# A transformer pair in split fp32r: moving the start addresses of the turned activations and of the fp32r tensors

## The chip, the cores and the metric

The kernel runs on one core of one Trainium2 chip. The metric is the time of one execution on the device in microseconds, as the median of several executions. Distances between addresses are given in bytes within a partition of SBUF.

## The reference

Two transformer layers on 256 tokens of width 1024, all in fp32. Cut to what matters here:

```python
def first_block(x, ...):                      # layer 1
    h = x
    h = h + 0.5 * swiglu(rms_norm(h, ffn1_norm), ffn1_w_gu, ffn1_w_down)      # ffn_a
    h = h + hybrid_mixer(rms_norm(h, mix_norm), w_in, ..., w_out)             # NSA and HGRN2
    h = h + 0.5 * swiglu(rms_norm(h, ffn2_norm), ffn2_w_gu, ffn2_w_down)      # ffn_b
    return rms_norm(h, final_norm)
def swiglu(x, w_gu, w_down):
    gate, up = jnp.split(x @ w_gu, 2, axis=-1)                                # width 2752
    return (jax.nn.silu(gate) * up) @ w_down
# second_block: two layers of FFN, attention (first FoX, then MLA), FFN (ffn_c to ffn_f),
# each followed by a layer norm, and a gated per-layer embedding behind each layer
```

## The kernel before

**Numbers.** Each matmul in fp32 is made of three in fp32r: an operand is split in a high part (a rounded copy) and a low part (the rest), and hi·hi, hi·lo and lo·hi are summed in PSUM. Weights come by DMA in chunks of 128 x 3072 floats into four buffers `w_raw`; ScalarE writes the high part into one of two buffers `w_hi` (line 407), VectorE the low part into one of two `w_lo` (line 414).

**Turned activations.** There are norm stages n = 0 to 11. After each but the last, TensorE turns the 256 x 1024 activations (line 492), ScalarE writes the high parts (line 736) and VectorE the low parts (line 849). Stages 0 to 7, 9 and 10 all write the same tensor `xT`, of 8 k-tiles x (high, low) x 256 tokens, so a k-tile's high and low part stand side by side (2,048 bytes); stage 8 writes `o2_hi`, `o2_lo` (`mla_oT`). An FFN f = a to f reads the stage n = 0, 2, 3, 5, 7, 9; the mixer's projections read n = 1, FoX n = 4, the gates of the embeddings n = 6 and 10, MLA's shared keys n = 7; MLA keeps the outputs of heads 0 to 7 in `xT`.

**What TensorE does with it.** The stationary operand is loaded by an instruction of its own ahead of its matmul; the other operand moves.

- FFN, tiles 1 to 20 of 22 (and tile 0 for c, d, e): `feature_major_twice`, once for gate and once for up. Weights are stationary, `xT` moves. Per k: `lo` weights against the high part (256 columns, line 451, or 454 for k = 0), and `hi` weights against high and low together (512 columns, line 452). So one tile is 16 matmuls of 512 columns and 16 of 256, which alternate. Then come the 12 matmuls of 512 columns of the tile before it that multiply by w_down (`token_major`, line 462): `hT_hi` or `hT_lo` is stationary, weights move. Late tiles of b to f put off half of this and use copies, `held_w_*` and `held_hT_*`.
- `feature_major` (line 441): weights stationary, 256 columns of `xT`, or of `mla_cqT`/`mla_ckvT`, move. It serves the projections of the mixer, FoX and MLA and the last tile of each FFN.
- `token_major` (line 462) with `xT`, `mix_oT`, `fox_oT`, `mla_oT` stationary, weights moving: output projections, gates, values.
- `block_tokens`, `pe_first` and `first_tile` (lines 506 to 513, 564 to 568, 588 to 591): the first products behind a norm.

**Order.** Each engine runs its own list, written out by hand (`pe_program` and the like), with semaphores between them.

**Where tensors lie.** They are placed one behind another in the order of declaration, each padded to 32 bytes: 4 `w_raw`, 2 `w_hi`, 2 `w_lo` (12,288 bytes each), `x`, `xn` (8,192 each), `xT` (16,384), `gains` (8,192), `const` (11,008), three of 1,024, then `hT_hi0`, `hT_hi1`, `hT_lo0`, `hT_lo1` (1,024 each), five small ones (160 bytes with their padding), `small` (256), and behind that what each stage brings of its own: `mix_oT_*` or `fox_oT_*` first; in MLA `ckvT_hi`, `ckvT_lo` (2,048 each), `k_rope` (1,024), the gains (2,560), `stat` (32), `oT_hi`, `oT_lo` (8,192 each), `cqT_hi`, `cqT_lo` (3,072 each). The held copies begin 29,824 bytes behind `hT_lo1`: `held_w_hi`, `held_w_lo` (8,192 each), `held_between` (776 floats), four `held_hT_*`.

Of the kernel before, what the change touches and what calls it, by code (L numbers as in the profile page):

```python
# [246 lines left out]


def build(nc, t, out):
    with ExitStack() as ctx:  # L250
# [40 lines left out]
        xT = sb("xT", [P, KD, 2, SEQ], F32R)  # L291
        xT_hi, xT_lo = xT[:, :, 0, :], xT[:, :, 1, :]
# [21 lines left out]
        small = sb("small", [P, 64])  # L314
# [130 lines left out]
        def feature_major_twice(o, hi, lo, col):  # L445
# [49 lines left out]
        def pe_first(n, src, i, tiles):  # L495
# [3 lines left out]
            front, back = range(KD // 2), range(KD // 2, KD)  # L499

# [70 lines left out]
        def pe_ffn(f, n, src):  # L571

            at = first[FFN[f]]

# [19 lines left out]
            def gate_up(i):  # L594
# [91 lines left out]
        def pe_features(i, tiles, signal, a_hi=None, a_lo=None, k_tiles=KD, n=None, col=None):  # L686

            hi, lo = w_hi[chunks[i].pair], w_lo[chunks[i].pair]
            wait_split(pe, i)
            for j, (o, free) in enumerate(tiles):  # L690
                pe.wait_ge(*free)
                feature_major(o, hi, lo, col or (lambda k: (len(tiles) * k + j) * P), k_tiles, a_hi or xT_hi, a_lo or xT_lo,
                              range(k_tiles)).then_inc(signal, 1)

        def pe_tokens(i, width, tiles, signal):

            wait_split(pe, i)
# [6 lines left out]
        def act_squares(n, src, mean, blocks=range(TB)):  # L704

            for b in blocks:
                for half in range(2):
# [9 lines left out]
                    elif n in PLE_NORM:  # L717
                        aside = xT_hi[:, 4 * half:4 * half + 4, tok_of(b)]
# [7 lines left out]
        def turned_views(n, p):  # L726
# [3 lines left out]
            return [z[:, k0:k0 + 4, tok_of(b)] for z in ((o2_hi, o2_lo) if n == 8 else (xT_hi, xT_lo))] + [bank[:, :].rearrange("p (k t) -> p k t", t=P)]  # L730
# [318 lines left out]
        def pe_mixer():  # L1049
# [3 lines left out]
            pe_tokens(first["nsa_v"], VSW, [(bank(3, VSW), none), (bank(4, VSW), none)], mix_tile)  # L1053
            pe_tokens(first["hg_g"], SEQ, [(bank(5), none), (bank(6), none)], mix_tile)
            pe_tokens(first["hg_g"] + 1, SEQ, [(bank(7), none), (bank(0), (nsa_copied, 1))], mix_tile)
# [16 lines left out]
            pe_features(place["hg_fq", 0], [(bank(2), (nsa_copied, 3)), (bank(3), (nsa_copied, 4))], mix_tile)  # L1072
            pe_features(place["hg_fq", 1], [(bank(4), (nsa_copied, 5)), (bank(5), (gate_made_hg, 1))], mix_tile)
            compressed(0)
            pe_features(place["hg_fq", 2], [(bank(6), (gate_made_hg, 2)), (bank(7), (gate_made_hg, 3))], mix_tile)
            compressed(1)
            pe_features(place["hg_fq", 3], [(bank(0), (gate_made_hg, 4)), (bank(2), (fk_sig_made, 1))], mix_tile)
            compressed(2)
            pe_tokens(place["hg_v", 0], SEQ, [(bank(3), (q_made, 1)), (bank(4), (fk_sig_made, 2))], mix_tile)
            compressed(3)  # L1080
            pe_tokens(place["hg_v", 1], SEQ, [(bank(5), (q_made, 2)), (bank(6), (fk_sig_made, 3))], mix_tile)
            pe_features(first["nsa_b"], [(bank(7), (q_made, 3)), (bank(0), (fk_sig_made, 4)), (bank(2), (q_made, 4))], mix_tile)
# [7 lines left out]
            pe_features(first["nsa_c"], [(bank(4), (hv_copied, 2)), (bank(5), (hv_copied, 3))], mix_tile)  # L1090
# [585 lines left out]
        def pe_fox():  # L1676
            none = (fox_tile, 0)

            f, v = first["fox_f"], first["fox_v"]
            pe_turn(4, x, (0, 1))  # L1680
# [4 lines left out]
            pe_features(f, [(psum[4][:, 0:SEQ], none)], fox_tile)  # L1685
            block_tokens(4, v + 1, SEQ, psum[3][:, 0:SEQ], 1, xT_hi, xT_lo).then_inc(fox_tile, 1)
            tiles = lambda f0, f1: [(psum[7][:, 0:SEQ], f0), (psum[6][:, 0:SEQ], f1)]
            pe_tokens(v + 2, SEQ, tiles(none, none), fox_tile)
# [4 lines left out]
            pe_tokens(first["fox_v"] + 3, SEQ, tiles((fox_v_made, 5), (fox_v_made, 6)), fox_tile)  # L1693
# [185 lines left out]
        with ExitStack() as scope:  # L1879
# [6 lines left out]
            lat_stat = lt("stat", [P, 2 * TB, 2])  # L1886
# [24 lines left out]
        def mla_out(h):  # L1911
            hi, lo = (xT_hi, xT_lo) if h < KD else (o2_hi, o2_lo)
            return hi[:, h % KD, :], lo[:, h % KD, :]

        def pe_shared_kv():

            pe_tokens(first["kv_down1"], KL, [(psum[b][:, 0:KL], (added, 4 * 7 + 2)) for b in range(TB)], mla_tile)
            pe_turn(8, x, (0, 1))
            pe_features(first["kv_down2"], [(psum[2 + j][:, 0:SEQ], (added, 4 * 7 + 4)) for j in range(2)], mla_tile)
            pe_turn(8, x, (2, 3))  # L1920

        def pe_mla():
# [88 lines left out]
            def rest(c, b, half):  # L2011
# [9 lines left out]
                if b == 0:  # L2021
                    pe.wait_ge(att_lo, A0 + min(3 * c + 3, MLA_H))

            pe_out(("mla_o1", "mla_o2"), lambda h: (xT_hi if h < KD else o2_hi)[:, h % KD, :],
                   lambda h: (xT_lo if h < KD else o2_lo)[:, h % KD, :], MLA_H, 3, ahead=rest)
# [644 lines left out]
```

## Time and profile before

| | |
|---|---|
| time, median of 3 executions | 1739.42 us (1739.07 to 1739.47) |
| profiled execution, first to last instruction (its span) | 1736.7 us |
| PE busy | 1674.9 us (96% of the span) |
| DVE busy | 1185.4 us (68%) |
| ACT busy | 873.0 us (50%) |
| HBM read and written | 173 GB/s over the span |

The profile is of one execution; of its own time only the span is given, and what lies before the first and behind the last instruction is not in it. PE is TensorE's matmuls, PEld its weight loads, DVE VectorE, ACT ScalarE, POOL GpSimd. The end of a matmul is modelled, so that a matmul's duration reaches over the start of the next. What a matmul costs in a stream is therefore the distance from its start to the start of the next one; in the chain of waits, which gives to each instruction only its part of the path, a row "x12" with 2.72 us says just that of twelve.

### The profile page before, as it was taken

Reading aid. Unit: us, or ns where it says so; the run is one execution under the profiler, and the core shown is the slowest. Engines: PE = TensorE matmul, PEld = TensorE weight load, DVE = VectorE, ACT = ScalarE, POOL = GpSimd, SP = SyncE. Lnnn points to the kernel's source line nnn. Section 1 sums busy time; section 2 is a strip of 40 time slices with the busy share of each in tenths; the row PEclk is TensorE's granted clock in tenths of the full one; section 3 lists DMA queues with packets and bytes.
Section 4 is the critical chain, followed back from the end, with each engine's and each line's share of the span. In section 5 each row is a group of like instructions: output and inputs, shape, how many; then the busy total and the mean of one; then the engine's idle time right before and its main releaser. Section 6 shows DMA issues by size and latency. Waiting matters only on the chain.

```text
span 1736.7 us, 24477 instructions
## 1 busy us (share of the span) xinstructions
PE 1674.9 (96%) x9836; PEld 1450.7 (84%) x9836; DVE 1185.4 (68%) x1949; ACT 873.0 (50%) x1497; POOL 76.0 (4%) x115
## 2 busy tenths in 40 slices
PE   7999999999999999999999999989999999999997
PEld 6888798888888888888878888778889887888885
DVE  5666646966666776675877667766667675576676
ACT  4544455655444544445655444544445565454444
POOL 0000002201000000001200000000000000100000
PEclk9999999899999999999999999999999999999999
DMA  8545255024555455445436554545445333455541
GB/s 347 190 182 186 107 201 237 1 97 170 185 194 199 174 208 192 182 146 219 146 146 229 198 196 171 193 174 185 182 176 203 117 113 119 162 222 200 189 158 49
DMA packets 32113, 301.57 MB, mean 174 GB/s; under 512 B 3824, under 2 KB 4352, under 8 KB 6016
## 3 DMA queue, kind: packets, MB, share of 16 engines
q1 hardware_dynamic: 32000, 300.01, 46.6%
q8 instruction: 78, 1.28, 0.3%
q14 instruction: 35, 0.29, 0.1%
HBM read 298.93 MB, written 1.06 MB: 173 GB/s over the span
## 4 chain that ended last, share of the span: by engine, by line
PE 86%; DVE 7%; ACT 5%; issue 1%; POOL 0%; DMA 0%; SPq 0%; DVEq 0%; ACTq 0%
PE bank L462 29%; PE bank L452 26%; PE bank L451 11%; PE bank L441 8%; DVE w_lo L414 3%; PE bank L454 2%; ACT w_hi L407 1%; PE bank L589 1%; PE bank L492 1%; PE bank L1155 1%; PE bank L1106 1%; DVE xT L849 1%; PE bank L1123 0%; DVE x L819 0%; ACT bank L721 0%
## 5 line engine op out<-in xcount | busy, mean ns | idle before, releaser
L414 DVE TENSOR_TENSOR w_lo<-w_raw,w_hi 128x1024 fp32r<-128x1024 f32 (+5 forms) x535 | 593.9, 1159 | 215.0 <-ACT w_hi L407 214.3
L452 PE MATMUL bank<-xT,w_hi 128*128 128x512 f32 x1920 | 674.2, 396 | 0.6 <-DVE w_lo L414 0.6
L407 ACT ACTIVATE w_hi<-w_raw 128x1024 fp32r<-128x1024 f32 (+5 forms) x543 | 507.9, 995 | 115.6 <-PE bank L462 93.5
L451 PE MATMUL bank<-xT,w_lo 128*128 128x256 f32 x1680 | 468.5, 279 | 0.0
L452 PEld LDWEIGHTS bank<-xT,w_hi 128*128 128x128 f32 x1920 | 351.8, 188 | 70.4 <-DVE w_lo L414 1.0
L451 PEld LDWEIGHTS bank<-xT,w_lo 128*128 128x128 f32 x1680 | 316.9, 189 | 10.5
L767 ACT ACTIVATE ff_silu<-ff_silu 128x256 f32<-128x256 f32 x123 | 51.5, 419 | 390.6 <-DVE ff_silu L917 390.6
L462 PE MATMUL bank<-w_hi,hT_hi 128*128 128x512 f32 x488 | 190.6, 391 | 0.5 <-DVE hT_lo L926 0.5
L462 PE MATMUL bank<-w_hi,hT_lo 128*128 128x512 f32 x488 | 189.9, 389 | 0.0
L462 PE MATMUL bank<-w_lo,hT_hi 128*128 128x512 f32 x488 | 189.9, 389 | 0.0
L917 DVE TENSOR_REDUCE ff_silu<-bank 128x256 f32<-128x512 f32 x123 | 84.9, 690 | 106.5 <-PE bank L452 105.1
L441 PE MATMUL bank<-xT,w_hi 128*128 128x256 f32 x672 | 123.6, 285 | 1.0 <-DVE w_lo L414 1.0
L462 PE MATMUL bank<-w_hi,xT 128*128 128x256 f32 (+2 forms) x448 | 107.9, 334 | 6.7 <-ACT mla_v L2053 2.6
L441 PEld LDWEIGHTS bank<-xT,w_hi 128*128 128x128 f32 x672 | 104.8, 191 | 5.7 <-issue 4.2
L462 PEld LDWEIGHTS bank<-w_hi,hT_lo 128*128 128x128 f32 x488 | 91.6, 188 | 19.7
L462 PEld LDWEIGHTS bank<-w_lo,hT_hi 128*128 128x128 f32 x488 | 91.6, 188 | 19.7
L462 PEld LDWEIGHTS bank<-w_hi,hT_hi 128*128 128x128 f32 x488 | 91.6, 188 | 15.6 <-issue 1.3
L441 PE MATMUL bank<-xT,w_lo 128*128 128x256 f32 x336 | 95.0, 283 | 0.0
L926 DVE TENSOR_TENSOR hT_lo<-ff_silu,hT_hi 128x256 fp32r<-128x256 f32 x122 | 51.9, 425 | 59.0 <-ACT hT_hi L773 59.0
L773 ACT ACTIVATE hT_hi<-ff_silu 128x256 fp32r<-128x256 f32 x122 | 50.9, 417 | 78.9 <-DVE ff_silu L924 78.9
L462 PEld LDWEIGHTS bank<-w_hi,xT 128*128 128x128 f32 x448 | 75.4, 190 | 16.3 <-issue 4.6
L918 DVE TENSOR_REDUCE ff_up<-bank 128x256 f32<-128x512 f32 x123 | 83.7, 680 | 0.0
(388 smaller groups left out, 2221.3 us busy)
## 6 DMA issues: line engine op xcount, KB each, us to landing
w_raw<-in_ffn_a SPq DMA_DIRECT2D x22, 1536.0 KB, 6.7
w_raw<-in_ffn_b SPq DMA_DIRECT2D x22, 1536.0 KB, 6.5
w_raw<-in_ffn_c SPq DMA_DIRECT2D x22, 1536.0 KB, 6.5
w_raw<-in_ffn_d SPq DMA_DIRECT2D x22, 1536.0 KB, 6.5
w_raw<-in_ffn_e SPq DMA_DIRECT2D x22, 1536.0 KB, 6.4
w_raw<-in_ffn_f SPq DMA_DIRECT2D x22, 1536.0 KB, 6.3
gains<-in_gains SPq DMA_DIRECT2D x11, 1024.0 KB, 4.8
w_raw<-in_mla_up SPq DMA_DIRECT2D x8, 1280.0 KB, 5.7
```

Source lines behind the costliest of these rows:

```text
L407: nc.scalar.activation(hi, src, ACTF.Copy).then_inc(w_hi_made, 1)
L414: nc.vector.tensor_tensor(lo, src, hi.bitcast(F32), ALU.subtract).then_inc(w_lo_made, 1)
L441: ins = nc.tensor.matmul(o, w[:, c], a[:, k, :], start=(n == 0), stop=(n == last))
L451: nc.tensor.matmul(o[:, 0:SEQ], lo[:, c], xT[:, k, 0, :], start=False, stop=False)
L452: ins = nc.tensor.matmul(o, hi[:, c], xT[:, k, :, :], start=(k == 0), stop=(k == KD - 1))
L454: nc.tensor.matmul(o[:, 0:SEQ], lo[:, c], xT[:, k, 0, :], start=False, stop=False)
L462: ins = nc.tensor.matmul(o, a(k)[:, tok_of(b)], w[:, c], start=(first_k and n == 0), stop=(last_k and n == 3 * len(ks) - 1))
L767: nc.scalar.activation(sig[s][r, :], gate[r, :], ACTF.Silu).then_inc(silu_made, 1)
L773: nc.scalar.activation(hT_hi[z][r, :], sig[s][r, :], ACTF.Copy).then_inc(h_hi_made, 1)
L917: nc.vector.tensor_reduce(sig[s][:, :], gate.rearrange("p (two s) -> p s two", two=2), AX_X, ALU.add).then_inc(gate_summed, 1)
L918: m = dve_own.step(nc.vector.tensor_reduce(up_sum[:, :], up.rearrange("p (two s) -> p s two", two=2), AX_X, ALU.add))
L926: nc.vector.tensor_tensor(hT_lo[z][r, :], sig[s][r, :], hT_hi[z][r, :].bitcast(F32), ALU.subtract).then_inc(h_lo_made, 1)
```

## The change

`xT` becomes a room of 128 floats more, and each stage n takes its own view of the room, `TURNED_AT[n]` floats behind the room's start: 64 bytes for n = 0, 128 for n = 2, 192 for n = 1, 3, 4, 6 and 10, 256 for n = 5, 320 for n = 7, 384 for n = 9. All that reads or writes `xT` takes the view of its stage; MLA's heads 0 to 7 take that of n = 9. The tensors behind the room move by 512 bytes. `small` grows by 32 bytes, `held_between` by 32, `lat_stat` by 32, so that `mix_oT`, `fox_oT`, `ckvT`, `held_hT`, the embeddings' `pT` copies, `mla_oT` and `cqT` begin at multiples of 64 bytes. No instruction is added, removed, resized or put at another place, and no wait changes.

```diff
+TURNED_AT = {0: 16, 1: 48, 2: 32, 3: 48, 4: 48, 5: 64, 6: 48, 7: 80, 9: 96, 10: 48}
+TURNED_ROOM = 128
...
-        xT = sb("xT", [P, KD, 2, SEQ], F32R)
-        xT_hi, xT_lo = xT[:, :, 0, :], xT[:, :, 1, :]
+        xT_room = sb("xT", [P, 2 * KD * SEQ + TURNED_ROOM], F32R)
+        def turned_x(n):
+            a = TURNED_AT[n]
+            return xT_room[:, a:a + 2 * KD * SEQ].rearrange("p (k two s) -> p k two s", k=KD, two=2)
+        def turned_hi_lo(n):
+            return turned_x(n)[:, :, 0, :], turned_x(n)[:, :, 1, :]
...
-            sb("held_between", [P, 776], on=held)
+            sb("held_between", [P, 784], on=held)
...
-        small = sb("small", [P, 64])
+        small = sb("small", [P, 72])
...
-                    feature_major_twice(gate, hi, lo, lambda k: 2 * P * k)
-                    feature_major_twice(up, hi, lo, lambda k: 2 * P * k + P).then_inc(gate_up_made, 1)
+                    feature_major_twice(gate, hi, lo, lambda k: 2 * P * k, turned_x(n))
+                    feature_major_twice(up, hi, lo, lambda k: 2 * P * k + P, turned_x(n)).then_inc(gate_up_made, 1)
...
-            lat_stat = lt("stat", [P, 2 * TB, 2])
+            lat_stat = lt("stat", [P, 2 * TB, 4])
...
-            hi, lo = (xT_hi, xT_lo) if h < KD else (o2_hi, o2_lo)
+            hi, lo = turned_hi_lo(9) if h < KD else (o2_hi, o2_lo)
```

## Rows read from the trace of the kernel before

**Rows 1.** The page: busy time of the engines, and PE's largest matmul groups.

```profile
PE 1674.9 (96%) x9836; PEld 1450.7 (84%) x9836; DVE 1185.4 (68%) x1949; ACT 873.0 (50%) x1497; POOL 76.0 (4%) x115
...
L452 PE MATMUL bank<-xT,w_hi 128*128 128x512 f32 x1920 | 674.2, 396 | 0.6 <-DVE w_lo L414 0.6
L451 PE MATMUL bank<-xT,w_lo 128*128 128x256 f32 x1680 | 468.5, 279 | 0.0
```

**Rows 2.** The chain that ended last, whole span, by line.

```profile
by line: PE bank L462 28.8%; PE bank L452 25.8%; PE bank L451 11.3%; PE bank L441 8.1%; DVE w_lo L414 2.8%; PE bank L454 1.6%; ACT w_hi L407 1.3%; PE bank L589 1.1%; PE bank L492 0.8%; issue 0.8%; PE bank L1155 0.6%; PE bank L1106 0.5%; DVE
```

**Rows 3.** Windows of ffn_b, ffn_c and FoX: stretch, its length, each engine's busy time.

```profile
core 0: us, PE busy (x) PEld busy (x) DVE busy (x) ACT busy (x) POOL busy (x), PEclk, DMA share, GB/s
410.00:584.00 174.00, 173.70 (x946) 149.81 (x944) 119.09 (x150) 82.49 (x111) 0.00 (x0) 1.00 0.53 197
606.00:765.00 159.00, 159.00 (x846) 136.40 (x845) 110.46 (x136) 75.74 (x99) 0.00 (x0) 1.00 0.51 184
828.00:865.00 37.00, 37.00 (x308) 32.93 (x304) 30.25 (x86) 25.69 (x76) 11.14 (x20) 1.00 0.48 171
```

**Rows 4.** The chain in order of time, an FFN tile's down part, twice: start, us, what.

```profile
438.04 2.72 PE bank L462 x12
446.35 2.72 PE bank L462 x12
```

**Rows 5.** Timeline of PE, gate (from 440.60) and up (from 443.41) of one tile.

```profile
440.60 0.39 PE L452 MATMUL bank<-xT,w_hi 128*128 128x512 f32 x1
440.82 0.28 PE L454 MATMUL bank<-xT,w_lo 128*128 128x256 f32 x1
...
443.18 0.63 PE L452 MATMUL bank<-xT,w_hi 128*128 128x512 f32 x2
443.65 0.28 PE L454 MATMUL bank<-xT,w_lo 128*128 128x256 f32 x1
...
446.19 0.39 PE L462 MATMUL bank<-w_hi,hT_hi 128*128 128x512 f32 x1
```

**Rows 6.** The chain: streams of 256 columns with `xT` moving (mixer, FoX, ffn_d's last tile).

```profile
238.82 11.52 PE bank L441 x96
828.33 3.07 PE bank L441 x24
1081.28 5.75 PE bank L441 x48
```

**Rows 7.** Timeline of PE: a stream of 256 columns with `mla_cqT` moving, first and tenth.

```profile
1401.08 0.28 PE L441 MATMUL bank<-mla_cqT_hi,w_lo 128*128 128x256 f32 x1
...
1402.10 0.28 PE L441 MATMUL bank<-mla_cqT_hi,w_lo 128*128 128x256 f32 x1
```

**Rows 8.** The chain: 512 columns, stationary `mix_oT`, `fox_oT`, `held_hT` mostly, `xT` with `mla_oT`.

```profile
386.86 16.11 PE bank L462 x69
891.84 14.26 PE bank L462 x60
1087.03 11.25 PE bank L462 x48
1471.94 25.42 PE bank L462 x111
```

**Rows 9.** The waits of PE: line waited for, us in total, times, longest.

```profile
PE bank L589 <- DVE xT L849: 10.1, 6, 5.2
PE bank L482 <- DMA const<-in_const: 8.5, 1, 8.5
PE bank L506 <- DVE w_lo L414: 4.8, 3, 1.8
```

More of the change, by code:

```diff
@@ L443, in feature_major, with feature_major_twice @@
             return ins
-        def feature_major_twice(o, hi, lo, col):
+        def feature_major_twice(o, hi, lo, col, xT):
             for k in range(KD):
@@ L691, in pe_features, with pe_tokens @@
                 pe.wait_ge(*free)
-                feature_major(o, hi, lo, col or (lambda k: (len(tiles) * k + j) * P), k_tiles, a_hi or xT_hi, a_lo or xT_lo,
-                              range(k_tiles)).then_inc(signal, 1)
-        def pe_tokens(i, width, tiles, signal):
+                feature_major(o, hi, lo, lambda k: (len(tiles) * k + j) * P, KD, xT_hi, xT_lo, range(KD)).then_inc(signal, 1)
+        def pe_tokens(n, i, width, tiles, signal):
+            xT_hi, xT_lo = turned_hi_lo(n)
             wait_split(pe, i)
@@ L728, in turned_views @@
             k0, bank = 4 * half, psum[4 + 2 * b + half]
-            return [z[:, k0:k0 + 4, tok_of(b)] for z in ((o2_hi, o2_lo) if n == 8 else (xT_hi, xT_lo))] + [bank[:, :].rearrange("p (k t) -> p k t", t=P)]
+            return [z[:, k0:k0 + 4, tok_of(b)] for z in ((o2_hi, o2_lo) if n == 8 else turned_hi_lo(n))] + [bank[:, :].rearrange("p (k t) -> p k t", t=P)]
         def act_turn(n, pieces=range(4)):
@@ L1679, in pe_fox @@
             f, v = first["fox_f"], first["fox_v"]
+            xT_hi, xT_lo = turned_hi_lo(4)
             pe_turn(4, x, (0, 1))
@@ L1692, in pe_fox @@
             ins.then_inc(cum_turned, 1)
-            pe_tokens(first["fox_v"] + 3, SEQ, tiles((fox_v_made, 5), (fox_v_made, 6)), fox_tile)
+            pe_tokens(4, first["fox_v"] + 3, SEQ, tiles((fox_v_made, 5), (fox_v_made, 6)), fox_tile)
             def project(p, part):
@@ L1911, in mla_out @@
         def mla_out(h):
-            hi, lo = (xT_hi, xT_lo) if h < KD else (o2_hi, o2_lo)
+            hi, lo = turned_hi_lo(9) if h < KD else (o2_hi, o2_lo)
             return hi[:, h % KD, :], lo[:, h % KD, :]
         def pe_shared_kv():
-            pe_tokens(first["kv_down1"], KL, [(psum[b][:, 0:KL], (added, 4 * 7 + 2)) for b in range(TB)], mla_tile)
+            pe_tokens(7, first["kv_down1"], KL, [(psum[b][:, 0:KL], (added, 4 * 7 + 2)) for b in range(TB)], mla_tile)
             pe_turn(8, x, (0, 1))
-            pe_features(first["kv_down2"], [(psum[2 + j][:, 0:SEQ], (added, 4 * 7 + 4)) for j in range(2)], mla_tile)
+            pe_features(7, first["kv_down2"], [(psum[2 + j][:, 0:SEQ], (added, 4 * 7 + 4)) for j in range(2)], mla_tile)
             pe_turn(8, x, (2, 3))
@@ L2022, in rest @@
                     pe.wait_ge(att_lo, A0 + min(3 * c + 3, MLA_H))
-            pe_out(("mla_o1", "mla_o2"), lambda h: (xT_hi if h < KD else o2_hi)[:, h % KD, :],
-                   lambda h: (xT_lo if h < KD else o2_lo)[:, h % KD, :], MLA_H, 3, ahead=rest)
+            pe_out(("mla_o1", "mla_o2"), lambda h: mla_out(h)[0], lambda h: mla_out(h)[1], MLA_H, 3, ahead=rest)
         def act_latents(js):
```

35 lines of the change are left out of this document (20 added, 15 removed).

## The prediction

> **What bounds the kernel now.** I read the page first, for the engines' shares, then the chain of waits by line, then windows over three stages, then the timeline of single matmuls. PE is busy 96% of the span [rows 1], but a busy PE is no proof of a full one. The chain confirms it: its largest parts are PE's lines 462, 452, 451 and 441, together 74.0% of the span, 452, 451 and 454 alone 38.7% [rows 2]. In the windows over ffn_b, ffn_c and FoX PE has no idle time worth naming, DVE is busy 119.09 of 174.00 us or 30.25 of 37.00, ACT less, and DMA about half [rows 3]. All PE waits over 4 us in one group sum to 23.4 us, at the start and behind norms [rows 9]. So a nanosecond off the distance between two matmul starts, in those streams, comes off the end; and these streams have cover: DVE would be the limit in an FFN only when a tile shrinks to 119.09/174.00 = 68% of its length.
>
> How far are the streams from full? The granted clock is 1.00 in these windows [rows 3], the 2.4 GHz level. At one column a cycle 512 columns are 213.3 ns and 256 are 106.7 ns. An FFN tile repeats every 446.35 - 438.04 = 8.31 us, of which the 12 down matmuls have 2.72 us [rows 4], 226.7 ns each, 13.3 ns over their columns. Gate lasts 2.81 us and up 2.78 us [rows 5], where 8 x (213.3 + 106.7) would be 2.56. Over the whole span the chain's 38.7% are 672.1 us for 1,920 matmuls of 512 columns [rows 1] and as many of 256; their columns are 614.4 us. The excess is **57.7 us, 15.0 ns a matmul**, or 30.1 ns a pair.
>
> **Is the excess a matter of addresses?** The instructions stay the same, so this is the whole question. Take the distance between the start of the next stationary operand, which is loaded while a matmul runs, and the start of what moves in that matmul, modulo 512 bytes (every slice of a tensor here begins at a multiple of 512 in it). From the sizes in the section on the kernel: `xT` lies 4 x 12,288 + 2 x 8,192 bytes behind `w_hi0`, so weights against `xT` have distance 0, in every stage. `hT` lies 38,656 bytes behind `xT`: 256. `cqT` lies 67,264 behind it: 192 ahead of the weights. `mix_oT` and `fox_oT`: 160, no multiple of 64. `mla_oT`: 192. `held_hT` against `held_w`: 32.
>
> Now compare. With `xT` moving 96 matmuls of 256 columns take 11.52 us, 120.0 ns each [rows 6]. With `cqT` moving, the same line and shape, nine take 1.02 us, 113.3 ns [rows 7]. The excess halves, 13.3 to 6.7 ns. What differs is the operand's tensor: 192 bytes of distance instead of 0, and a k-step of 1,024 bytes instead of 2,048. In 512 columns, the stage of `fox_oT` has 14.26 us for 60 and that of `held_hT` 11.25 for 48, 237.7 and 234.4 ns; `xT` with `mla_oT` has 25.42 for 111, 229.0 [rows 8]; down 226.7 [rows 4]. Rows that end a stage hold the last matmul's drain, some 0.16 us (390 ns of duration less 227 of distance), which takes 60 to 235.0 and 111 to 227.6; the misaligned tensors still stand 4 to 8 ns over down's 226.7. So distance matters, and 0 is not the best of them. I take distance as the cause and the k-step as a rival.
>
> A rule speaks against all of it. The Trainium skill, "TensorE: Matmul & The Clock Gate", section "Step-by-step: what each phase is for", says that TensorE has two independent read ports, and that loading the next tile's weights takes no bandwidth from the running matmul. By that rule start addresses change nothing and the time stays at 1739.4; by the rows the same shape has two prices, 120.0 and 113.3, and the sum below follows. The trace does not agree with the rule as it stands; it is rival B2.
>
> **The change part by part.**
>
> 1. FFN gate and up, tiles in `feature_major_twice`: 320 pairs in each of six FFNs. The distance goes from 0 to 64, 128, 192, 256, 320, 384 bytes of `xT` ahead of the weights in a, b, c, d, e, f. Best case from rows: 6.7 ns on the 256 [rows 7] and 13.3 on the 512, the least that rows of 512 show [rows 4]. That is 1,920 x 20.0 = 38.4 us of excess, so 19.3 us less, 3.2 an FFN. (Were 6.7 reached on both: 25.6, so 32.1 less; that is the lower bound.) For c, at the 192 of `cqT`, I take the whole 3.2. For the other five no row has this alternation at their distance; between nothing and 3.2 I take 40%, 1.3 each, as 512-column streams at distances 256 and 192 show 226.7 and 228.5 [rows 4, 8] and nothing below. Sum: 3.2 + 6.5 = **-9.7**. The upper bound is that an alternation gets dearer: case C below.
> 2. Line 441 with `xT` at 192: mixer 4 x 48 + 72 + 48 = 312 matmuls, FoX 24 + 8 x 48 = 408. 720 x 6.7 = **-4.8** (between 0 and -4.8; FoX's window has no idle [rows 3], and its 3.07 us for 24 hold the same 120 beside an entry). The last tiles of the FFNs, 240 matmuls now at 119.8 [rows 6]: 40% of 240 x 6.7, **-0.6**.
> 3. Stationary `mix_oT`, `fox_oT`, 96 each, from 160 to 192: 192 x 5.5 ns (235.0, and 16.11 for 69 [rows 8] less its drain, 231.2, both to 227.6) = **-1.1**. Held down matmuls, about 48 in each of five FFNs, 234.4 to some 230: 240 x 4 = **-1.0**. `pT`, 24 each, and `ckvT`: nothing.
> 4. `cqT` goes from 192 to 256. 288 matmuls, at worst back to 120.0, +1.9; half: **+0.9**. `xT` stationary in gates and MLA's output goes from 0 to -192 or -384: about 288 matmuls by 1.8 ns (if `xT`'s half of the 111 [rows 8] cost down's 226.7, `mla_oT`'s cost 228.5): **+0.5**. The products of 128 columns and the value products: 0, with +-1 us.
> 5. DVE, ACT and DMA touch the same bytes in the same number. Their work is hidden in the FFNs anyway. If each of the some 160 instructions that write or read `xT` outside PE became 50 ns longer, half of them on the path, +4 us; nothing in the trace suggests it, so 0.
>
> Sum: -9.7 - 4.8 - 0.6 - 1.1 - 1.0 + 0.9 + 0.5 = **-15.8 us**. It is made against the span of 1736.7; the median of the runs is 2.7 more, which does not change. 1739.4 - 15.8 = **1723.6**.
>
> **The rivals.**
>
> B1, distance does nothing. The cheaper `cqT` comes from its k-step of 1,024 bytes, or from which tensors alternate, and not from the distance. Then parts 1, 2 and 4 are 0 and part 3 leaves -1 to -2: about 1738. For: there is just one tensor at 192 with a k-step of its own, and the streams of down at 256 and of `xT` at 0 in 512 columns are equally dear. Against: the misaligned rows.
>
> B2, loads and moving reads do not meet at all, and what looks like misalignment comes from which tensors follow each other. Then every part is 0 and the time stays at 1739.4. Against it stand the 4 to 8 ns of part 3 and the 6.7 of part 2, for it only that no row changes an address and nothing else. It is what the rule of the Trainium skill named above would give.
>
> C, slower. A shift brings the moving operand's later reads onto the weight load, where at distance 0 they ran in step. The price is in rows too: a 512-column matmul beside a badly placed stationary operand takes 235.0 [rows 8] where the alternation's now takes 672.1 us x 25.8/38.7 / 1,920 = 233.4, so little; but if the 256s stay at 120 and the 512s go to 240, a pair takes 360 against 350.1, +3.2 us an FFN. With five FFNs so, and parts 2 to 4 at -3, 1739.4 + 16 - 3 = about 1752. It outweighs the rest from two to three bad FFNs on when no other gains. Against it: distance 0, where both operands start in step, should be the worst, and the one other distance in 256 columns is better.
>
> D, only 192 helps: c -3.2, part 2 -4.8, part 3 -2.1, part 4 +1.3, the other FFNs 0: 1730.6. It is on the same side as the forecast.
>
> E, it all reaches 6.7: -32.1 -6.4 -2: 1699. All six distances would have to be good.
>
> **How the numbers follow.** Forecast (most FFNs gain something) 0.52, D 0.22, E 0.06: faster. B1 0.06, of which 0.03 is just outside 0.2% on the faster side; B2 0.03. C 0.11, of which 0.02 nets out to nothing. 0.2%, 3.5 us, is about what this kernel's measurement can tell from no change: faster 0.83, within it 0.08, slower 0.09. The likeliest case alone runs from 1713 to 1729. The range for 8 in 10 takes in D and B1 and leaves out E and most of C: 1709 to 1738.
>
> **What would show it.** Right, step by step: line 451's and 452's chain share falls from 38.7% of the span; the FFN tile's period differs between FFNs, with ffn_c near 8.31 - 0.16 = 8.15 us; down stays 2.72 us; line 441 with `xT` in mixer and FoX goes to 113.3 ns (96 in 10.9 us); the 60 of `fox_oT` fall below 14.0 us. Wrong: a period of 8.31 us in all six FFNs is B1 or B2; one above 8.31 in any is C's mechanism; line 441 still at 120.0 says the k-step made `cqT` cheap; an FFN with new PE idle time would say that DVE had no room. The prediction fails most easily in the 40% of part 1, which no row prices.

## The result, and the profile after

The changed kernel takes 1740.97 us, the median of 12 runs (1738.67 to 1742.32); the kernel before, run on the same chip, takes 1737.09 us (12 runs, 1735.53 to 1739.47). The ratio is 1.0018, with a 95% interval of [1.0011, 1.0025]: some 3 us slower, where 15.8 us less were forecast. (Here and below, the ratio compares executions that were taken side by side; it is near the quotient of the two medians, but not equal to it.) The profiled executions differ by 2.4 us in span (1739.1 against 1736.7).

The page after, the engines' busy time, and then the chain that ended last, by line. The lines of before 441, 451, 452, 454 and 462 are now 452, 462, 463, 465 and 473.

```profile
PE 1675.8 (96%) x9836; PEld 1449.9 (83%) x9836; DVE 1185.6 (68%) x1949; ACT 873.1 (50%) x1497; POOL 75.8 (4%) x115
```

```profile
by line: PE bank L473 28.9%; PE bank L463 25.7%; PE bank L462 11.5%; PE bank L452 8.0%; DVE w_lo L425 3.0%; PE bank L465 1.6%; ACT w_hi L418 1.2%; PE bank L603 1.1%; issue 0.9%; PE bank L503 0.8%; DVE xT L864 0.5%; PE bank L1170 0.5%; PE ba
```

PE is as busy as before [rows 1]. Gate and up have 25.7 + 11.5 + 1.6 = 38.8% of a longer span, where they had 38.7% [rows 2]: the forecast saving is absent.

The windows of ffn_b, ffn_c and FoX, with the columns of [rows 3].

```profile
410.00:584.00 174.00, 173.68 (x933) 149.09 (x932) 119.45 (x150) 83.28 (x112) 0.00 (x0) 1.00 0.54 198
606.00:765.00 159.00, 159.00 (x838) 135.95 (x838) 109.37 (x136) 74.35 (x97) 0.00 (x0) 1.00 0.50 181
828.00:865.00 37.00, 37.00 (x316) 32.79 (x315) 31.32 (x88) 26.12 (x80) 11.55 (x20) 1.00 0.48 171
```

PE's idle time and the clock are as before; the counts are not. In ffn_b and ffn_c fewer matmuls start in the same stretch (933 against 946, 838 against 846), in FoX more (316 against 308). So the distance between two starts has changed, up in the one place and down in the other. A few per cent of the records can be missing, so the periods are read from the chain.

The chain in order of time: the down part of two tiles that follow each other, in b, c and d. The difference of the two starts is the period, to be held against [rows 4].

```profile
427.66 2.76 PE bank L473 x12
436.01 2.76 PE bank L473 x12
...
624.01 2.74 PE bank L473 x12
632.39 2.74 PE bank L473 x12
...
1020.79 2.72 PE bank L473 x12
1029.10 2.72 PE bank L473 x12
```

Over all tiles of a stage the period is 8.39 us in a (64 bytes ahead), 8.35 in b (128), 8.37 in c (192), 8.31 in d (256), 8.39 in e (320), 8.35 in f (384). Against 8.31 that is 20 tiles x (0.08 + 0.04 + 0.06 + 0 + 0.08 + 0.04), 6 us more. Of that, 0.02 to 0.04 us a tile lie in the 12 down matmuls, whose operands moved by 512 bytes against the weights in every stage alike, and which still take 2.72 us in d: their price came to depend on what ran ahead of them.

Where a tile pays shows in the mean distance from one start to the next, worked out from all such matmuls of a stage in both traces (ns, before to after; the first column is line 451, now 462):

```
stage, lead     256 columns       512 columns       down (three groups)
a, 64          116.0 to 119.5    233.5 to 233.9    227.2 to 228.7
b, 128         116.0 to 118.7    233.6 to 231.2    227.1 to 229.9
c, 192         115.9 to 117.8    233.5 to 233.9    227.1 to 228.6
d, 256         116.0 to 115.9    233.5 to 233.5    227.1 to 227.1
e, 320         116.0 to 119.4    233.5 to 233.9    227.1 to 228.7
f, 384         116.0 to 118.7    233.5 to 231.2    227.1 to 230.1
```

In a, c and e the 256s got dearer by 1.9 to 3.5 ns and the 512s by 0.4; in b and f the 512s got 2.4 cheaper, the 256s lost as much again, and the whole loss is in down. The page's mean durations go the same way: 281 ns for the 256s of line 462 after, where line 451 had 279 [rows 1].

The chain in the mixer (96) and MLA (a stream with `mla_cqT`, 36), and the groups of 512 columns of [rows 8].

```profile
238.62 10.89 PE bank L452 x96
...
385.08 15.83 PE bank L473 x69
...
889.78 14.00 PE bank L473 x60
...
1084.74 11.18 PE bank L473 x48
...
1374.82 4.58 PE bank L452 x36
```

96 matmuls of 256 columns take 10.89 us instead of 11.52 [rows 6]: 113.4 ns each, as forecast. 69 and 60 take 15.83 and 14.00 instead of 16.11 and 14.26 [rows 8]. The six groups of 36 with `mla_cqT` took 4.39 to 4.41 us before, and take 4.58 to 4.60 now.

The 96 are not the whole of line 441's part. In FoX most streams have 24 matmuls and come in pairs, one from each half of a chunk of weights. A pair in the chain, before and then after:

```profile
836.77 3.07 PE bank L441 x24
840.64 3.07 PE bank L441 x24
```

```profile
835.67 2.92 PE bank L452 x24
839.39 3.03 PE bank L452 x24
```

By distance between starts the one stands at 113.3 to 114.0 ns after the change and the other at 117.8, with the same lead of 192 bytes. Over all streams of line 452 with `xT` moving the mixer has 115.7 ns in the mean (before 120.1) and FoX 115.6 (before 119.7), so only some two thirds of the forecast 6.7 ns were reached. Against that, streams that the prediction took as unchanged got cheaper: the value products of 256 columns, with `xT` stationary. One of them in the mixer, before and then after:

```profile
265.22 5.94 PE bank L462 x48
```

```profile
264.03 5.64 PE bank L473 x48
```

By starts 288 such matmuls in mixer and FoX went from some 119.8 ns to 113.3 (96 of them) or 117.8 (192), about 1.0 us in all.

Measured between the same matmuls of both traces, the stages have changed by +1.5 (a), -2.4 (mixer), +0.8 (b), +1.2 (c), -2.0 (FoX), -0.1 (d), +1.6 (e), +2.2 (MLA) and +0.8 us (f), the load at the start by -0.7; with the embeddings that sums to about +3, and the rest lies at the ends. The FFNs lose 5.8, mixer and FoX win 4.4.

MLA's last stretch holds a thing of another kind. The chain, first before, then after, where the product of 18 matmuls follows a time with many short waits; then the window over it, after.

```profile
1450.16 4.37 PE bank L462 x18
1455.51 4.11 PE bank L462 x18
```

```profile
1450.23 5.73 PE bank L473 x18
...
1456.94 4.18 PE bank L473 x18
```

```profile
1450.20:1456.00 5.80, 5.77 (x20) 4.63 (x21) 3.92 (x9) 3.74 (x6) 0.00 (x0) 0.75 0.31 130
```

The granted clock is 0.75 in the mean of that window, so that part of it ran at the 1.2 GHz level; 18 matmuls took 5.73 - 4.37 = 1.36 us longer. From 1441.00 to 1450.00 PE had been busy 6.57 of 9.00 us. In the kernel before the clock was 1.00 here, with PE busy 6.52 of the same 9.00, but fell in MLA's first stretch (0.50 from 1353.00 to 1356.00), where it is 1.00 after. Over the whole span both have about the same, 0.990 and 0.989. The next groups of 18, at the full clock, take 4.18 us instead of 4.11: 3.9 ns a matmul for `xT` as stationary operand at its new place.

### The profile page after: what moved, and what is told of

Read it like the earlier page. It is cut to its first block, busy times and chain, and to the rows that moved or that the text cites. A ratio compares the mean times of both kernels' runs of the same rounds, so it can differ in the third digit from the quotient of the medians.

```text
span 1739.1 us, 24477 instructions
## 1 busy us (share of the span) xinstructions
PE 1675.8 (96%) x9836; PEld 1449.9 (83%) x9836; DVE 1185.6 (68%) x1949; ACT 873.1 (50%) x1497; POOL 75.8 (4%) x115
## 4 chain that ended last, share of the span: by engine, by line
PE 86%; DVE 8%; ACT 4%; issue 1%; POOL 0%; DMA 0%; SPq 0%; DVEq 0%; ACTq 0%
PE bank L473 29%; PE bank L463 26%; PE bank L462 11%; PE bank L452 8%; DVE w_lo L425 3%; PE bank L465 2%; ACT w_hi L418 1%; PE bank L603 1%; PE bank L503 1%; DVE xT L864 1%; PE bank L1170 1%; PE bank L1121 0%; DVE x L834 0%; PE bank L518 0%; ACT bank L736 0%
```

## The experiments

In what follows the lead of a tensor is the number of bytes that it begins ahead of the weights, and of the distances only the remainder modulo 256 is told where nothing else is said. Before the change `xT` has lead 0. The chain's tile periods are named "period".

**One half of the change at a time.** The first kernel keeps the alignment (the 32 bytes more of `small`, `held_between` and `lat_stat`), with all views of `xT` at lead 0; the second keeps the views, without the alignment.

```diff
-TURNED_AT = {0: 16, 1: 48, 2: 32, 3: 48, 4: 48, 5: 64, 6: 48, 7: 80, 9: 96, 10: 48}
+TURNED_AT = {0: 0, 1: 0, 2: 0, 3: 0, 4: 0, 5: 0, 6: 0, 7: 0, 9: 0, 10: 0}
```

> All views of xT at the room's start (distance 0 as in the kernel before), the 64-byte alignment of the other tensors kept. Theory (distance modulo 256 bytes sets the price of a matmul): all six FFN tiles have the period of before, 8.31 us; line 441 with xT moving 120.0 ns in the mixer and FoX; mla_cqT, which alignment put at 256 bytes from the weights, costs 119.7 ns as in the changed kernel and not 114.7, +1.3 us; mix_oT and fox_oT at 192 instead of 160 save about 1 us. Sum within 1.5 us of the kernel before. Rival (the alignment itself costs the 5.9 us that the FFNs lost): the periods of 8.39 and 8.35 us stay, and the time is 1741 or more.

It took 1739.17 us (10 runs) against 1738.22 (19 runs of before): 1.0012 [1.0002, 1.0021]. The chain of its profile:

```profile
238.18 11.52 PE bank L452 x96
386.20 15.83 PE bank L473 x69
1374.72 4.58 PE bank L452 x36
```

The 96 with `xT` moving are as dear as before. The 69 and the 36 have their values of after, and so have the 60, 14.00 us: these three belong to the alignment. All FFN periods are 8.31 us.

```diff
-            sb("held_between", [P, 784], on=held)
+            sb("held_between", [P, 776], on=held)
...
-        small = sb("small", [P, 72])
+        small = sb("small", [P, 64])
...
-            lat_stat = lt("stat", [P, 2 * TB, 4])
+            lat_stat = lt("stat", [P, 2 * TB, 2])
```

> The shifted views, without the 64-byte alignment of small, held_between and lat_stat. Theory: FFN periods as in the changed kernel (8.39, 8.35, 8.37, 8.31, 8.39, 8.35 us), line 441 at 115 to 116 ns in the mixer and FoX, mla_cqT back at 192 bytes and so at 114.7 ns; MLA gets back about 1.3 us, mix_oT and fox_oT lose 1: 1740 +- 1.5. Rival: as for the run with alignment alone, the FFNs return to 8.31 us and the time falls below 1735.

It took 1738.68 us (10 runs) against 1738.22: 1.0012 [1.0002, 1.0021] once more. The six periods are those of the changed kernel to 0.01 us, and the 36 with `mla_cqT` take 4.40 us again. So the loss in the FFNs is the views' alone. Neither half by itself brings a gain.

**Is it the distance or the FFN?** The same views, dealt out to other FFNs: a 256 bytes, b 192, c 448, d 64, e 128, f 512.

```diff
+TURNED_AT = {0: 64, 1: 48, 2: 48, 3: 112, 4: 48, 5: 16, 6: 48, 7: 32, 9: 128, 10: 48}
```

> The changed kernel with other shifts in the FFNs: a 256 bytes, b 192, c 448, d 64, e 128, f 512. Theory (distance of weights to xT modulo 256 bytes, whatever the FFN): the period follows the shift: a 8.313, b 8.373, c 8.373 (448 is 192 modulo 256), d 8.393, e 8.353, f 8.313 us. Rival 1 (it belongs to the FFN, its banks or its neighbours): a stays at 8.393, d at 8.313. Rival 2 (modulo 512 bytes or more): a and f differ, and b and c differ.

One execution, 1739.77 us. The chain in d (64 bytes):

```profile
945.25 2.74 PE bank L473 x12
953.64 2.74 PE bank L473 x12
```

The periods are 8.31 (a), 8.37 (b), 8.37 (c), 8.39 (d), 8.35 (e), 8.31 (f). Each distance took its price along into another FFN, 192 and 448 bytes have the same, and 256, 512 and 0 have the same. The period hangs on the distance modulo 256, and not on the stage.

**Distances between the multiples of 64.** Leads 16 (a), 32 (b), 48 (c), 96 (d), 160 (e), 224 (f).

```diff
+TURNED_AT = {0: 4, 1: 48, 2: 8, 3: 12, 4: 48, 5: 24, 6: 48, 7: 40, 9: 56, 10: 48}
```

> The changed kernel with shifts in the FFNs that are no multiples of 64 bytes: a 16 bytes, b 32, c 48, d 96, e 160, f 224. Theory (lines of 64 bytes: a start inside a line touches one more): all six at or above 8.35 us, none below before's 8.313. Rival (finer steps matter, and a small step of 16 or 32 bytes lets the two reads run beside each other): one of them falls below 8.30 us, which would be a gain of 0.3 us or more in that FFN.

One execution, 1733.97 us. The chain in a (16):

```profile
105.71 2.72 PE bank L473 x12
113.98 2.72 PE bank L473 x12
```

The periods are 8.27, 8.31, 8.34, 8.35, 8.29 and 8.38 us. The theory that no lead goes below 8.31 fell: 16 bytes save 0.04 us a tile, 160 bytes 0.02.

Leads 240 (a), 8 (b), 144 (c), 112 (d), 176 (e), 208 (f), and `xT` at 16 in mixer and FoX:

```diff
+TURNED_AT = {0: 60, 1: 4, 2: 2, 3: 36, 4: 4, 5: 28, 6: 48, 7: 44, 9: 52, 10: 48}
```

> The changed kernel with other shifts of fine grain: xT in a 240 bytes ahead of distance 0, b 8, c 144, d 112, e 176, f 208; mixer and FoX 16. Theory (a function of the distance modulo 256 bytes, with steps of 16 bytes, in which a small lead of xT is cheap): b between 8.27 us (the 16 bytes of the run before) and 8.313; a, the other side of 0, above 8.31; line 441 at 16 bytes of lead below 120.0 ns. Rival (it was luck of that one FFN's state): b at 8.31 or above, and line 441 at 120.0.

One execution, 1740.61 us. Periods 8.42, 8.35, 8.31, 8.33, 8.36 and 8.37. The expectation that 8 bytes would share in the gain of 16 fell; half the step makes a tile dearer than lead 0 does. Line 452 in the mixer takes 116.6 ns in the mean of its five streams at lead 16, 115.7 at 192 and 120.1 at 0; in FoX it is 116.8, 115.6 and 119.7. The 96 take 10.88 us at lead 16 and 10.89 at 192. So for streams of 256 columns 16 is about as good as 192, and 1 ns dearer in the mean.

**The alternation taken apart.** In gate and up all seven remaining matmuls of 512 columns come behind all eight of 256, at leads 0 (a), 16 (b), 64 (c), 128 (d), 192 (e), 160 (f).

```diff
+            c0 = slice(col(0), col(0) + P)
+            nc.tensor.matmul(o, hi[:, c0], xT[:, 0, :, :], start=True, stop=False)
             for k in range(KD):
                 c = slice(col(k), col(k) + P)
-                if k:
-                    nc.tensor.matmul(o[:, 0:SEQ], lo[:, c], xT[:, k, 0, :], start=False, stop=False)
-                ins = nc.tensor.matmul(o, hi[:, c], xT[:, k, :, :], start=(k == 0), stop=(k == KD - 1))
-                if k == 0:
-                    nc.tensor.matmul(o[:, 0:SEQ], lo[:, c], xT[:, k, 0, :], start=False, stop=False)
+                nc.tensor.matmul(o[:, 0:SEQ], lo[:, c], xT[:, k, 0, :], start=False, stop=False)
+            for k in range(1, KD):
+                c = slice(col(k), col(k) + P)
+                ins = nc.tensor.matmul(o, hi[:, c], xT[:, k, :, :], start=False, stop=(k == KD - 1))
```

> feature_major_twice in another order: hi weights for k = 0, then all eight lo weights (256 columns), then hi weights for k = 1 to 7 (512 columns), so that equal lengths follow each other; the same sums in another order. Lead of xT over the weights: a 0 bytes, b 16, c 64, d 128, e 192, f 160. Theory (each length has its own best distance, and the alternation mixed a gain and a loss): the 256s cost 120.0 ns in a and 113.3 to 116 in e as in line 441's streams, and the 512s 226.7 in a as in down's and more in the others; gate and up together in a 16 x 120.0 + 16 x 226.7 = 5.55 us and a period of 8.27 us, 0.04 below before's. Rival (a matmul's price hangs on its distance alone, not on its neighbours): the period in a stays 8.313, in b 8.273, in c 8.373, in d 8.353, in e 8.393.

One execution, 1739.90 us. The chain of a product in a (lead 0), and of one in e (lead 192):

```profile
127.37 0.95 PE bank L463 x8
128.32 1.61 PE bank L466 x7
...
1263.15 0.92 PE bank L463 x8
1264.07 1.63 PE bank L466 x7
```

From lead 0 to lead 192 the eight of 256 columns get cheaper, 0.95 us to 0.92, and the seven of 512 dearer, 1.61 to 1.63. Between single starts inside these groups the 256s stand at 120 ns at lead 0 and at 113 to 115 at 192. The seven 512s have 230.6 ns in the mean at lead 0, but the last two of them 226.7; at 192 they have 232.4 in the mean, and go to and fro between 231 and 236 to the end. At lead 128 they take 232.6, at 64 230.5. In streams of one shape, then, one distance is good for the 256s and bad for the 512s, where seven in a row are too few to show the steady price. The expected 8.27 us in a was not reached for the same reason: the order gave 8.31 there, and 8.34, 8.31, 8.38, 8.31 and 8.39 in the others. Against the alternation that is 0.08 less in c (lead 64), 0.06 less in e (192), and more in b (16), d (128) and f (160), by 0.07, 0.03 and 0.10, so the sequence matters as well as the distance.

**Down, by itself.** `xT` at lead 0, the four tensors of `hT` moved by 16 bytes (a), 32 (b), 64 (c), 128 (d), 192 (e), 240 (f) from a distance that is 0 modulo 256. In down `hT` is the stationary operand.

```diff
-        hT_hi = [sb(f"hT_hi{i}", [P, SEQ], F32R) for i in range(2)]
-        hT_lo = [sb(f"hT_lo{i}", [P, SEQ], F32R) for i in range(2)]
+        hT_room = [sb("hT", [P, 4 * SEQ + 64], F32R)]
...
+        HT_AT = (4, 8, 16, 32, 48, 60)
+
+        def hT_view(f, s, low):
+            a = HT_AT[f] + (2 * low + s % 2) * SEQ
+            return hT_room[s // 2][:, a:a + SEQ]
```

> xT at distance 0 in all FFNs; instead hT, the stationary operand of the down matmuls, is placed apart in each FFN: 16, 32, 64, 128, 192, 240 bytes further than before (where its distance to the weights is 256, or 0 modulo 256) in a to f. Theory (distance modulo 256 bytes sets the price here too, and a lag of the moving operand is dear): down takes 2.72 us for 12 where it is unchanged, and more at 64, 128 and 192, some 228 to 236 ns each as with mla_oT and mix_oT; gate and up stay at 5.59 us less what the first ones inherit. Rival (only the streams of lines 451 and 452 are sensitive): 2.72 us in all six.

One execution, 1741.95 us. The chain in a (16 bytes):

```profile
106.38 2.80 PE bank L477 x12
114.78 2.80 PE bank L477 x12
```

Twelve take 2.80, 2.80, 2.80, 2.80, 2.75 and 2.74 us, all more than the 2.72 of [rows 4]; 2.80 / 12 = 233.3 ns against 226.7. So down, with the operands' parts exchanged, is as sensitive, and stood at the best place tried already.

**Each shape at its own distance.** `w_hi`'s part for gate and up, and for the streams of line 441 with `xT`, lies 64 bytes behind, so that `xT` at lead 0 against `w_lo` has lead 192 against `w_hi`; for the value products it lies 192 bytes behind; down keeps its distances.

```diff
-        w_hi = [sb(f"w_hi{i}", [P, CHUNK], F32R) for i in range(2)]
+        w_hi_room = [sb(f"w_hi{i}", [P, CHUNK + 64], F32R) for i in range(2)]
...
+        def hi_of(c, a=0):
+            at = (64 if a >= GU else 16) if c.name in FFN else HI_AT.get(c.name, 0)
+            return w_hi_room[c.pair][:, at:at + CHUNK]
```

> xT unshifted; instead w_hi gets rooms of 64 floats more, and the high weights of gate, up and of line 441's chunks lie 64 bytes behind distance 0 (xT leads them by 192 modulo 256), w_lo stays at 0; the high weights of down lie at 0 again. Value chunks have w_hi 192 further. mla_cqT stays at 192, mla_oT, held_hT come to 0. Theory (the price is set by the length of the matmul that runs and the distance between what it moves and the weights that load beside it): 512 columns run beside a load of w_lo at 0, 226.7 ns; 256 columns beside a load of w_hi at 192, 113.3 ns; a tile is 2.72 + 16 x 340.0 ns = 8.16 us, 120 tiles save 18 us; line 441 in mixer and FoX at some 115.5 ns saves 3; about 1717. Rival (what counts is a matmul's distance to its own weights): 256 at 120.0, 512 at 233.3, a tile 8.37 us, and the time 1744.

It took 1734.62 us (8 runs) against 1739.20 (14 runs): 0.9976 [0.9967, 0.9986]. All periods are 8.33 us, neither the 8.16 of the theory nor the 8.37 of the rival. The timeline of single matmuls in a gate product:

```profile
506.26 0.39 PE L470 MATMUL bank<-xT,w_hi 128*128 128x512 f32 x1
506.49 0.28 PE L469 MATMUL bank<-xT,w_lo 128*128 128x256 f32 x1
506.61 0.39 PE L470 MATMUL bank<-xT,w_hi 128*128 128x512 f32 x1
```

A pair starts every 506.61 - 506.26 = 0.35 us, as at lead 0; about 0.12 of it belong to the 256s and 0.23 to the 512s. The price of the alternation is not the sum of the two streams' best prices (113.3 + 226.7 = 340.0). By their starts the 256s have 117.6 ns and the 512s 232.1, 349.7 together where they had 349.5 before; the 0.02 us a tile lie in down, 228.4 ns in the mean against 227.0. Between the same matmuls as above, mixer and FoX are 2.0 and 1.5 us shorter than before, the start and ffn_a 1.2 each, the other FFNs mostly 0.3 to 0.4 longer. In ffn_a it is the first tile alone that is shorter, by the clock (see the next run); its later tiles lose as the others do. The 96 of the mixer went from 120.0 to 117.8 ns by a move of `w_hi` alone (`xT` moved by 512 bytes, which changes nothing modulo 256), so the address of the moving operand by itself does not set the price. Why the alternation settles at 8.33 is open.

**The best views together.** `xT` at lead 16 in all FFNs, at 192 in the feature products of mixer and FoX, at 0 in the gates; `mix_oT`, `fox_oT`, `mla_oT`, `held_hT`, `ckvT` and `pT` at 0; `mla_cqT` at 192, where it was before.

```diff
-HELD_AT = 29824
+HELD_AT = 29952
...
-TURNED_AT = {0: 16, 1: 48, 2: 32, 3: 48, 4: 48, 5: 64, 6: 48, 7: 80, 9: 96, 10: 48}
-TURNED_ROOM = 128
+TURNED_AT = {0: 4, 1: 48, 2: 4, 3: 4, 4: 48, 5: 4, 6: 0, 7: 4, 9: 4, 10: 0}
+TURNED_ROOM = 64
...
-            sb("held_between", [P, 784], on=held)
+            sb("held_between", [P, 832], on=held)
...
-        small = sb("small", [P, 72])
+        small = sb("small", [P, 88])
...
-            lat_stat = lt("stat", [P, 2 * TB, 4])
+            lat_stat = lt("stat", [P, 2 * TB, 16])
+            lt("below_cq", [P, 48])
```

> The best of the views alone, no change to w_hi: xT leads by 16 bytes in all FFNs, by 192 in mixer and FoX, by 0 in the gates; mla_cqT stays at 192 from the weights; mix_oT, fox_oT, mla_oT, held_hT at 0 modulo 256. Theory: all FFN tiles at 8.27 us (-0.04 x 120 = -4.8), mixer and FoX -4.5 as in the changed kernel, output matmuls -1.5, heads 0 to 7 in MLA's output +0.7: 1728 +- 2, against 1737 to 1738 before. Rival (the 8.27 us of one FFN needs what comes before it in that FFN): only ffn_a has it, and the time is 1732 or more.

It took 1729.16 us (6 runs) against 1739.20 (14 runs): 0.9935 [0.992, 0.995]. One of the six executions took 9382.99 us, for a reason that is not known, and is left out of the ratio; without it the median is 1729.11. The chain:

```profile
235.32 10.89 PE bank L452 x96
383.43 15.67 PE bank L473 x69
500.24 2.72 PE bank L473 x12
508.51 2.72 PE bank L473 x12
884.37 13.87 PE bank L473 x60
1366.46 4.39 PE bank L452 x36
```

All six periods are 8.27, the 96 stay at 10.89, the 69 and 60 fall by a further 0.16 and 0.13 us (lead 0 instead of 192 for the stationary operand), and `mla_cqT` is back at 4.39. Between the same matmuls the six FFNs are 5.6 us shorter than before (20 x 6 x 0.04 = 4.8 of it by their periods), mixer and FoX 3.3, and MLA 1.2 longer, of the spans' 8.8 in all (1736.7 - 1727.9). These parts are not all the addresses' doing, as the windows over ffn_a's first tile show, first before and then with the best views:

```profile
24.00:29.00 5.00, 5.00 (x28) 4.82 (x27) 3.35 (x4) 3.25 (x5) 0.00 (x0) 0.66 1.01 365
```

```profile
24.00:29.00 5.00, 5.00 (x37) 4.66 (x36) 3.89 (x6) 4.48 (x6) 0.00 (x0) 1.00 1.01 385
```

In the trace of before the granted clock fell for 3.4 us here and in this one it did not, which is 1.7 us of the FFNs' 5.6; 0.7 are lost again between ffn_d and ffn_e, around a fall at 1127 us. In the mixer it is the other way round: a fall at 284 us that before does not have makes 48 matmuls take 7.31 us, where the changed kernel has 5.71, and one at 1441 costs MLA about 1.6. Over the span the mean clock is 0.990 in both, so the 8.8 us are not the clock's; only their division over the stages is blurred by it. Matmuls of ffn_b by shape, the mean duration as the last number ahead of the idle time, first before and then with the best views:

```profile
L452 PE MATMUL bank<-xT,w_hi 128*128 128x512 f32 x320 | 112.4, 396 | 0.3 <-DVE w_lo L414 0.3
L451 PE MATMUL bank<-xT,w_lo 128*128 128x256 f32 x280 | 78.1, 279 | 0.0
```

```profile
L463 PE MATMUL bank<-xT,w_hi 128*128 128x512 f32 x320 | 111.4, 390 | 0.4 <-DVE w_lo L425 0.4
L462 PE MATMUL bank<-xT,w_lo 128*128 128x256 f32 x280 | 78.7, 281 | 0.0
```

The 512s are shorter by 6 ns and the 256s longer by 2. By distance between starts the 512s go from 233.6 to 227.2 ns, the 256s from 116.0 to 119.8, and down stays at 227: what lead 16 gives comes from the 512s alone. The kernel is faster than before and after, and its time (1728 +- 2) was foreseen from the prices that the earlier runs had shown, though one of these, 4.5 us for mixer and FoX, held more than line 441 (see above).

**The part that was right, alone.** The kernel before, with `xT` at 192 in the feature products of mixer and FoX and nothing else.

```diff
+TURNED_AT = {0: 0, 1: 48, 2: 0, 3: 0, 4: 48, 5: 0, 6: 0, 7: 0, 9: 0, 10: 0}
```

> The kernel before with one part of the change: xT 192 bytes further in the mixer and FoX alone (n = 1 and 4), every other view at 0, no alignment. Theory (192 helps streams of 256 columns and harms streams that hold 512s): FFN tiles 8.313 us, line 441 with xT 115 to 116 ns in mixer and FoX, mla_cqT 114.7; the 4.5 us that the changed kernel gained there stand alone: 0.9974 of the time before, -4.5 +- 1 us. Rival (the gain is eaten by VectorE and ScalarE, which set the pace between those streams): less than 2 us.

It took 1733.77 us (11 runs) against 1736.60 (15 runs): 0.9986 [0.9976, 0.9996], or -2.4 us with -0.7 to -4.2. The expected -4.5 is just outside. In the trace the mixer is 2.1 us and FoX 1.7 us shorter, 3.8 together. (The spans differ by more, 5.1 us, of which some 1.5 are ffn_a's first tile, where the clock did not fall in this trace either.) The chain shows the forecast price in the 96:

```profile
236.55 10.89 PE bank L452 x96
```

Over all streams of line 452 with `xT` moving the distances are as in the changed kernel, 115.7 ns in both stages. The sign is shown, the size only to that interval.

**Close to 16 bytes.** The kernel of the best views with leads 12 (a), 20 (b), 24 (c), 28 (d), 40 (e), 56 (f).

```diff
+TURNED_AT = {0: 3, 1: 48, 2: 5, 3: 6, 4: 48, 5: 7, 6: 0, 7: 10, 9: 14, 10: 0}
```

> The best views with other leads of xT in the FFNs: a 12 bytes, b 20, c 24, d 28, e 40, f 56. Theory (16-byte steps with the good place at 16): a above 8.273 us as 8 bytes was (8.353), the starts inside the second 16 bytes (20, 24, 28) between 8.27 and 8.36, none below 8.273. Rival (a better place lies between 16 and 32): b, c or d below 8.26 us.

One execution, 1735.92 us. The chain in b (20 bytes) and in d (28):

```profile
449.56 2.72 PE bank L473 x12
458.00 2.72 PE bank L473 x12
...
944.58 2.73 PE bank L473 x12
952.85 2.73 PE bank L473 x12
```

Periods 8.29, 8.44, 8.42, 8.27, 8.35 and 8.40. The theory that the price goes in steps of 16 bytes fell: 4 bytes from the best lead lies the dearest of all.

Over these runs the period of an alternating tile, by lead:

```
lead    0    8    12   16   20   24   28   32   40   48   56   64
us     8.31 8.35 8.29 8.27 8.44 8.42 8.27 8.31 8.35 8.34 8.40 8.39
lead   96   112  128  144  160  176  192  208  224  240
us     8.35 8.33 8.35 8.31 8.29 8.36 8.37 8.37 8.38 8.42
```

## Why the prediction was wrong, step by step

**Is the excess a matter of addresses? Right.** Nothing but addresses differs between the kernels, and periods differ by up to 8.44 - 8.27 = 0.17 us a tile. That refutes B2, and the runs do not agree with the rule of the Trainium skill, "TensorE: Matmul & The Clock Gate", section "Step-by-step: what each phase is for", as far as it says that a weight load takes nothing from the running matmul. Down with its stationary operand 16 bytes further pays 233.3 ns against 226.7. B1 is refuted by the same pair and by the 96 matmuls at 113.4: with `xT` and its k-step of 2,048 bytes they reach the price of `mla_cqT`, so the k-step did not make that one cheap. The period of the effect was taken as 512 bytes; it is 256, as 64 and 320, 128 and 384, 192 and 448, and 0, 256 and 512, cost the same, while 0 and 128 do not. That the distance counts, and not the two addresses each by itself, is argued: moving `xT`, `w_hi` or `hT` alone each changed a price, and no run moves both operands of a matmul together.

**Part 1, the step that failed: FFN gate and up, forecast -9.7, measured +6.** The prediction carried prices of streams of one shape over to the alternation, an excess of 6.7 ns on the 256s (`mla_cqT`'s) and of 13.3 on the 512s (down's, at another distance), and gave c "the whole 3.2". In ffn_c each tile got 0.06 us longer instead. Three things were missed. The excess was taken as an even 15.0 ns a matmul, where 9.3 lie on the 256s (116.0 - 106.7) and 20.2 on the 512s, which starts in the trace of before could have told. Distances have opposite prices: without the alternation lead 192 wins 6 to 7 ns on the 256s and loses 2 on the 512s in the mean of seven, and 4 to 9 on the last two. And a price found in a stream does not hold in the alternation at all: at 192 its 256s went up, from 115.9 to 117.8, where the stream's went down. The 40% for the other five FFNs were an average over distances that no row priced; four of them lose, and one (256) is the same place as 0. Down, which the prediction expected to "stay 2.72 us", pays too, and in b and f it is down that loses. The saving that exists, 0.04 us a tile at the most, lies at 16 and at 28 bytes (12 and 160 save 0.02), which no multiple of 64 reaches. The sentence against C, that distance 0 "should be the worst", had no row behind it; 0 is the best of the multiples of 64.

**Part 2, line 441 in mixer and FoX, forecast -4.8: right in sign, and in price for part of the streams.** The 96, a 48 of the mixer and mostly one stream of each pair in FoX reached 113.3 to 114.0 ns where 113.3 were forecast; the others came to 115.4 to 118.5, most of them to 117.8. The means of 115.7 and 115.6 over 312 and 408 matmuls make 3.1 us of the 4.8. That the two stages still won 3.8 alone, and 4.4 with the alignment's part, is in some measure luck: 0.8 us of the one and 1.0 of the other came from the value products, which the prediction put at nothing. In the times of the features alone it is 2.4 [0.7, 4.2]. The last tiles of the FFNs (-0.6) gave some 0.2: 117.8 ns in a, c and e where they had 119.8, and 119.9 to 120.0 in b, d and f.

**Part 3, forecast -2.1: right in sign for one half, nothing in the other.** 0.28 us on 69 and 0.26 on 60 are 4.1 and 4.3 ns, which over 192 matmuls is 0.8 us (forecast 1.1). The held ones gave nothing (forecast 1.0). The row of 48 in [rows 8] holds only 36 of them, and 12 of the embedding with `ple_pT` stationary; in d, e and f the 36 take as long as before to 0.01 us, and the 0.07 us by which the row fell are the 12's.

**Part 4, forecast +1.4: too low for MLA.** `mla_cqT` at 256 is at the dear end, 0.19 us on 36 matmuls and 1.1 on six such groups (forecast 0.9 for all). `xT` as stationary pays 3.9 ns in the groups of 18 where 1.8 were taken, and the value products, put at 0, won (part 2).

**Part 5, DVE, ACT and DMA, forecast 0: right.** The windows show DVE at 119.45 us where it had 119.09, and no idle time of PE.

**The rivals.** C, with a chance of 0.11, was the case that came, in its sign and its place, the FFN tile, but not in its working: it had the 512s go to 240 ns with the 256s left at 120. The 512s stayed at 233.9 or fell, the 256s and down took the loss, and it is 6 us over six FFNs where 16 over five were put. Mixer and FoX gave 4.4 us of it back. D and E needed gains in the FFNs at distances where none are.

**What stays open.** MLA grew by 2.2 us, of which 1.1 is `mla_cqT` and up to 1.36 the fall of the granted clock at 1450. This fall, at the same matmuls, is in the profiles of all the experiments but two, the leads 16 to 224 and the features alone; before has none there, but a fall of its own at 1353, which cost it about 0.2 us. As each kernel has one profile, whether the change brings the fall is not settled. It doesn't decide the sign of the result: the FFNs alone outweigh mixer and FoX. Why 16 and 28 bytes are good and 20 and 24 bad is not explained by any of the theories, nor why one stream at lead 192 settles at 113.3 ns and the next at 117.8.

## What to carry to other kernels

Where fp32r matmuls run back to back with a weight load beside each, read the distance between two starts for each shape and order of matmuls, and treat where the moving and the stationary operand begin, modulo 256 bytes, as a parameter of its own: here it is worth 0.17 us in 8.3. A price that a stream of one shape shows at a distance is not to be carried over to another shape or to an alternation; try the place in the very stream, one value to each repeated stage of one kernel, as six FFNs gave six prices in one execution. For the alternation no multiple of 64 bytes was better than 0, and a tensor that is moved as an operand for one product must be costed in each part that it plays, moving and stationary.

## What the runs showed of the hardware that was not expected

A start 4 bytes further makes 16 of 8.27 us into 20 of 8.44. A stream's price also depends on what ran ahead of it: the same twelve down matmuls take 2.72 us in d and 2.76 in b and f, by `xT`'s place in the matmuls before them, and at a granted clock of 1.00 in both. Nor do addresses and shape together fix it: two streams of 48 matmuls in FoX, with one view of `xT` and one lead of 192, have 117.8 and 113.3 ns in the changed kernel, and 113.6 and 117.7, the other way round, in the kernel of the best views. The prices that come back most often for 256 columns are 113.3, 117.8 and 120.0 ns.

The Trainium skill, "SBUF — State Buffer", section "Who interferes with whom", gives PE two independent read ports, one for the moving operand and one for the weight load. No run here can see ports. What the runs show is that the place of the stationary operand sets a price, 2.80 us against 2.72 for the same twelve matmuls; that the two reads, or something that both need, meet is argued from it.

The same 18 matmuls took 4.37 us at a granted clock of 1.00 and 5.73 in a window of 0.75, behind 9.00 us in which PE was busy 6.57. Executions of one kernel spread with the clock: of the 15 of before that were taken beside the features alone, those with a mean clock of 0.994 or 0.995 took 1735.48 to 1736.34 us, those with 0.988 or 0.989 from 1736.34 up to 1739.83. That is as much as the whole effect of the change.
